# Modulation vectors of the next layer: the weighted sums moved from TensorE to GpSimd

## The reference, cut to what matters

```
silu_c  = silu(c)            # 1024 numbers, for the latent tokens
silu_cc = silu(c_ctx)        # 1024 numbers, for the context tokens
for i in range(4):
    mod_x = silu_c  @ w_mod[i] + b_mod[i]      # w_mod[i] is 1024 x 3072
    mod_c = silu_cc @ w_mod[i] + b_mod[i]
    shift, scale, gate = split(mod, 3)
    h = rms_norm(x, norm_g[i]) * (1 + scale) + shift
    ... mixer i ...
    x = x + gate * mixer_out
```

## Time and profile before

| | us |
|---|---|
| median of three runs | 8017.87 (8011.07 to 8035.23) |
| the profiled execution's own time | 8013.69 |
| its span, first to last instruction | 8011.9 |
| TensorE matmul busy | 6238.0, 78% |
| VectorE busy | 3114.6, 39% |
| ScalarE busy | 2047.2, 26% |
| GpSimd busy | 748.7, 9% |
| mean granted TensorE clock | 0.859 of full speed |

### The profile page before, as it was taken

How to read it: one execution, slowest core, us unless ns; L and a number is a source line. 1 busy time by engine, 2 the same in 40 slices (tenths; PEclk the granted TensorE clock), 3 DMA queues, 4 the chain that set the end, 5 groups by cost and what they waited for, 6 DMA issues and landing times. The chain is left out here.

```text
span 8011.9 us, 209544 instructions
## 1 busy us (share of the span) xinstructions
PE 6238.0 (78%) x90176; PEld 4264.4 (53%) x90176; DVE 3114.6 (39%) x7149; ACT 2047.2 (26%) x3566; POOL 748.7 (9%) x894
## 2 busy tenths in 40 slices
PE   5999777777778999888889350769699877777778
PEld 4555666666664555455445230544355566666664
DVE  3000455555551232255110689111310355555552
ACT  1000333333431111244011230210100244434440
POOL 0000222222220000000000000000000122222220
PEclk8999988888889899989988555569899988889988
DMA  3221000000002221221222305132111100000001
GB/s 104 85 91 68 25 16 16 16 16 16 16 8 100 86 88 61 79 63 43 100 78 85 48 31 45 47 76 83 64 71 66 43 16 16 16 16 16 16 16 63
DMA packets 172650, 401.84 MB, mean 50 GB/s; under 512 B 18752, under 2 KB 89280, under 8 KB 172224
## 3 DMA queue, kind: packets, MB, share of 16 engines
q1 hardware_dynamic: 137472, 297.39, 13.3%
q10 hardware_dynamic: 34752, 98.58, 3.0%
HBM read 286.86 MB, written 109.05 MB: 49 GB/s over the span
## 5 line engine op out<-in xcount | busy, mean ns | idle before, releaser
L278 PE MATMUL ps<-arena 128*128 128x512 f32 (+1 forms) x5824 | 2159.6, 533 | 249.6 <-DVE arena L1476 122.8
L278 PEld LDWEIGHTS ps<-arena 128*128 128x128 f32 x5824 | 1115.6, 192 | 1286.0 <-issue 1236.6
L1652 PE MATMUL ps<-arena 64*64 64x64 f32 x30720 | 639.2, 224 | 211.9 <-ACT arena L1924 119.6
L1652 PEld LDWEIGHTS ps<-arena 64*64 64x64 f32 x30720 | 549.8, 135 | 300.1 <-issue 293.1
L1924 ACT COPY arena<-ps 128x512 f32<-128x512 f32 (+1 forms) x800 | 497.6, 632 | 596.6 <-PE ps L1652 569.2
L486 PE MATMUL ps<-arena 128*128 128x512 f32 (+1 forms) x1152 | 425.5, 530 | 40.2 <-DMA arena<-na_w_in 40.2
L1982 POOL MEMSET arena<- 128x1024 f32 (+1 forms) x6 | 4.2, 739 | 4812.3 <-issue 4812.3
L1476 DVE SCALAR_TENSOR_TENSOR arena<-arena 128x1280 f32<-128x1280 f32 x96 | 141.3, 1547 | 635.4 <-PE ps L278 634.4
L1506 ACT COPY arena<-ps 128x1280 f32<-128x1280 f32 x64 | 78.4, 1225 | 1160.1 <-PE ps L278 1160.1
L486 PEld LDWEIGHTS ps<-arena 128*128 128x128 f32 x1152 | 220.8, 192 | 234.5 <-issue 223.3
L2104 DVE TENSOR_TENSOR arena<-ps,arena 128x512 f32<-128x512 f32 x480 | 302.5, 684 | 74.4 <-PE ps L1729 55.8
(11 more groups left out here) (252 smaller groups left out, 9954.3 us busy)
## 6 DMA issues: line engine op xcount, KB each, us to landing
proj<-arena ACTq DMA_DIRECT2D x104, 640.0 KB, 3.9
arena<-proj SPq DMA_DIRECT2D x104, 640.0 KB, 5.1
arena<-w_mod SPq DMA_DIRECT2D x96, 512.0 KB, 4.5
arena<-rw_w SPq DMA_DIRECT2D x68, 512.0 KB, 3.5
arena<-xres SPq DMA_DIRECT2D x40, 640.0 KB, 6.9
xres<-arena ACTq DMA_DIRECT2D x24, 640.0 KB, 6.5
arena<-na_w_in SPq DMA_DIRECT2D x24, 512.0 KB, 4.0
arena<-x SPq DMA_DIRECT2D x16, 640.0 KB, 6.7
```

The costliest lines, as they stand in the source:

```text
L278: last = nc.tensor.matmul(k.ps[:, 3 * u + n, 0:b - a], w[:, c * P:(c + 1) * P], src[:, c, a:b], start=(c == 0), stop=(c == KT - 1))
L1652: last = PE.matmul(part_of(out, dst, hh, g, d), part(l, src, hh, g, d), rhs, start=True, stop=True)
```

## The change

TensorE's eight two-column matmuls for a w_mod strip become two one-column matmuls. GpSimd first makes, for each of the two conditioning vectors, the weighted sum over the eight groups of input channels; TensorE sums that over the 128 partitions with a column of ones. GpSimd takes up the m strips of a turn when all m loads have landed, and TensorE's part waits for GpSimd (`weighted`) in place of the loads. A strip costs GpSimd twelve instructions and six drains: five multiplications (three over 4 x 128 elements of each partition, two over 2 x 128) and seven additions (one over 4 x 128, four over 2 x 128, two over 128). The second vector's products are written over the strip itself. SyncE's and VectorE's parts stay.

Besides, TensorE's program gets 153 `hold` instructions ahead of the recurrence's loop in layer 0 and 136 in layer 3.

```diff
 class HiddenModulation:
+        self.first, self.part, self.acc = k.arena.take(4, P), k.arena.take(2, P), k.arena.take(m, P)
+        self.weighted = es.semaphore("hm_weighted")
...
+    def pool_part(self, pool, i):
+        def times(out, strip, c, s):
+            n = out.shape[1]
+            self.nc.gpsimd.tensor_tensor(out, strip[:, c:c + n, :], self.k.cond[:, c:c + n, s:s + 1].to_broadcast([P, n, P]), ALU.mult)
+
+        def plus(out, a, b):
+            self.nc.gpsimd.tensor_tensor(out, a, b, ALU.add)
+
+        pool.wait_ge(self.w_in, i * (16 * self.m) + 16 * self.m)
+        hold(self.k, pool)
+        for q in range(self.m):
+            w = self.strips[:, q, :].rearrange("p (c o) -> p c o", o=P)
+            times(self.first, w, 0, 0)
+            times(self.part, w, 4, 0)
+            pool.drain()
+            plus(self.first[:, 0:2, :], self.first[:, 0:2, :], self.part)
+            pool.drain()
+            times(self.part, w, 6, 0)
+            pool.drain()
+            plus(self.first[:, 2:4, :], self.first[:, 2:4, :], self.part)
+            times(w[:, 0:4, :], w, 0, 1)
+            times(w[:, 4:8, :], w, 4, 1)
+            pool.drain()
+            plus(self.first[:, 0:2, :], self.first[:, 0:2, :], self.first[:, 2:4, :])
+            plus(w[:, 0:4, :], w[:, 0:4, :], w[:, 4:8, :])
+            pool.drain()
+            plus(self.acc[:, q, :], self.first[:, 0, :], self.first[:, 1, :])
+            plus(w[:, 0:2, :], w[:, 0:2, :], w[:, 2:4, :])
+            pool.drain()
+            plus(w[:, 0, :], w[:, 0, :], w[:, 1, :])
+        pool.drain().then_inc(self.weighted, 1)
+
     def tensor_part(self, pe, i):
-        pe.wait_ge(self.w_in, i * (16 * self.m) + 16 * self.m)
+        pe.wait_ge(self.weighted, i + 1)
         pe.wait_ge(self.ev, i + 1)
         for q in range(self.m):
-            for c in range(KT):
-                last = self.nc.tensor.matmul(self.k.ps[:, 6, 2 * q:2 * q + 2], self.strips[:, q, c * P:(c + 1) * P],
-                                             self.k.cond[:, c, :], start=(c == 0), stop=(c == KT - 1))
+            for s, sums in enumerate((self.acc[:, q, :], self.strips[:, q, 0:P])):
+                last = self.nc.tensor.matmul(self.k.ps[:, 6, 2 * q + s:2 * q + s + 1], sums, self.k.ones[:, 0:1], start=True, stop=True)
         last.then_inc(self.mm, 1)
...
 # in dense_to_dram, na_project and rwkv_project, each with its number of turns
+            @block.gpsimd
+            def _(pool):
+                with pool.Fori(0, turns) as i:
+                    hidden.pool_part(pool, i)
...
+LOOP_FILL = (153, 136)
...
 # in rwkv_recur
+            for _ in range(LOOP_FILL[j]):
+                hold(k, pe)
             pe.wait_ge(zeroed, 1)
             with pe.Fori(0, KT) as e:
```

More of the change, by code:

```diff
@@ L551, in _ @@
                 act.wait_ge(stored[u], 16 * 3 * KT // 2 + 16)
+        @block.gpsimd
+        def _(pool):
+            with pool.Fori(0, KT // 2) as pair:
+                hidden.pool_part(pool, pair)
         @block.vector
@@ L1454, in _ @@
                 turn(i)
+        if hidden:
+            @block.gpsimd
+            def _(pool):
+                with pool.Fori(0, hidden.turns) as i:
+                    hidden.pool_part(pool, i)
         @block.vector
```

## The result

The changed kernel takes 8091.74 us (median of 4 runs, 8084.70 to 8108.55), the kernel before beside it 8023.21 (4 runs, 8011.07 to 8035.23): ratio 1.0089, 95% interval 1.0066 to 1.0111. The profiled execution took 8084.70 us, that of before 8013.69: 71.0 more, at nearly the same mean clock (0.856 against 0.859).

What follows compares the result with a forecast made beforehand. The prediction took TensorE to bound the three projection phases. Layer 0's projection -25, `na_project` +107, S5 -26 and the fill +0.4 summed to +56 us on 8013.7; it said 8072 us, range 7985 to 8145.

Steps and rivals of the forecast that it cites:

- `na_project`: 16x16 attention's projection: GpSimd needs 65 us for six strips, TensorE waits 40 us a turn; +107 us in four turns.
- TensorE's saving in layer 0: Layer 0's projection: fewer matmul pairs save 31.4 us, a clock that stays up another 15; -46.4 us.
- The start: Layer 0's projection: GpSimd's first strips collide with VectorE's preparation, so TensorE starts 16 us later (ends: 0 and 20).
- The 5 us for turns in which VectorE makes `xs`: Layer 0's projection: in two turns GpSimd loses up to 12 us and uses up its margin; +5 us in all.
- A strip: GpSimd's cost for weighting one w_mod strip, drains included: 10.8 us, low end 7.8, high end 12.2.
- the 128x512 product near 1.28 us: Sign of being right: GpSimd's product of 512 elements per partition takes about 1.28 us; under 1 us would mean wrong.
- S5: S5's projection: GpSimd sets the pace with 32.4 us for three strips, turns of 40.3 us for 43.5; -26 us.
- The fill: Holds ahead of the recurrence's loops: 7.8 and 6.9 us, mostly covered by TensorE's wait for loads; +0.4 us.
- The recurrence's loop falls badly: Rival: moved instructions make all 64 recurrence windows as long as the first, 2.7 us each; +173, 8245 us; chance 0.04.
- dearer beside VectorE: Rival, `na_project`: VectorE's reciprocals hold GpSimd up, turns wait 8 to 16 us longer; 8105 to 8135; within the forecast's 0.68.
- no change: Rival: short GpSimd instructions cost less than their rows, a strip 9.7 us; 8019 us; chance 0.15.
- Faster: Rival: the repeated operand makes products cheaper, a strip under 8.9 us; 7981 us at 8.5; chance 0.13.

Runs made afterwards that it cites:

- e4: Changed kernel, with GpSimd in `rwkv_project` waiting for VectorE's first shifted copy before its first strip: 8093.29 us (one run).
- e3: Changed kernel, with `na_project`'s six w_mod strips issued after a turn's second row of weights instead of its last: 7928.73 us, ratio 0.9884 to the kernel before.
- e8: Changed kernel with holds under a wait, earlier `na_project` loads, later GpSimd start, and TensorE summing one of S5's three strips: 7876.85 us, 0.9812 of the kernel before.
- e2: Changed kernel, with the same holds moved to the head of TensorE's part of the projection, under an existing wait: 8054.69 us, ratio 1.0047 to the kernel before.

## Why the prediction was right

The forecast of 8072 us lay in the direction and of the size measured (8091.74), and the range held the result. The profiled executions differ by 71.0 us where the sum said 56. The mechanism that decides, GpSimd's lateness in `na_project`, is as forecast; that the total came so close is partly luck, since one term failed by 30 us and the others erred the other way. Point by point:

- **TensorE's saving in layer 0** held: -47.3 for -46.4, both parts of it, the fewer pairs and the clock that no longer falls.
- **The start** was +9.5 for +16. It was argued from rows of VectorE beside GpSimd, and the collision is there (2.04 us for 1.47), but the engines don't strictly alternate: VectorE loses 0.57 us an instruction where I took 0.82. With GpSimd held back (e4) the first strip is at 187.24 again, so the collision is the cause. The 5 us for turns in which VectorE makes `xs` didn't come: GpSimd lost 2.5 to 3.0 us there, not 12, and 8 us of margin held.
- **A strip** cost 10.04 to 10.4 us for 10.8, within 7%, by errors that partly cancel. The product was sized at 1.275 us and takes 1.04; the additions were sized at 1.098 and 0.644 and take 1.27 and 0.73. The rows I took the additions from read `eye2`, which repeats along the row: they were a cheaper form, and the product's row the dear one. The twelve instructions come to 9.4 us instead of 9.8, and the drains' gaps, less what neighbours overlap, to 0.6 instead of 1.0. The sign of being right "the 128x512 product near 1.28 us" failed. The Trainium skill's rate (GPSIMD Engine Reference, section 3.1) came to 9.4 us by the estimate, measured is 10.04. The additions here take 0.19 us and 2.11 ns an element, which at the section's 2048 elements would be 4.5 us, an estimate that agrees with its 4497 ns; what the estimate of 9.4 lacked is the fixed part.
- **`na_project`**: +96.2 for +107, with a wait of 36 us for 40, turns 24 us longer for 27, and GpSimd as the releaser. The six strips took 62.6 us for the 68 reckoned, but GpSimd began them 12.0 us after the first issue instead of 10.1. This was the deciding term, and e3 shows it as a cause: with the strips issued earlier the wait is gone and the term turns from +96.2 into -60.9 us (-67.5 + 6.6 at the phase's two ends against before).
- **S5**: -20.8 for -26, and +3.6 in phases behind it for which I had no term. I took the strips to land 5.7 us after their issue, every turn; it is 6.6 in the short turns and 9.1 to 10.7 in the long ones. That GpSimd sets the pace here held, and e8 shows it.
- **The fill is the step that failed.** "A `hold` takes 51 ns: 153 take 7.8 us" used the busy time of an instruction that stood alone as its pace in a row. In a row they come every 0.15 us: 23.3 us, of which 8.7 were covered, so +16.6 in layer 0 and +14.1 in layer 3, 30.7 in place of 0.4. e2 shows it as a cause: with the same holds under a wait the 31 us are gone. The other terms were too high together. From the 56 of the sum to the 71 measured: fill +30.3, S5 +5.2, `na_project` -10.8, start -6.5, layer 0's turns -5.9 (the 5 us that didn't come among them), and +2.6 for the stretches between.
- **"The recurrence's loop falls badly"** didn't happen in the changed kernel, and had 0.04. But the mechanism is real, its price is higher than I gave it (190 and 219 us in the two layers, not 173 for both), and it comes as a step, not as 2.7 us on every window. What I called a fill that "nearly restores the place" is what keeps 200 us away.

The rival "dearer beside VectorE" did not come as it was put: beside the reciprocals GpSimd ran at its own pace, and what it lost to VectorE's two-operand work was 2.4 us a turn, not 8 to 16. The rival "no change" was nearer than the result looks. It was given to strips of 8.9 to 10.1 us, and S5's take 10.04; by my own weights (24 us in each of the two phases for a microsecond of a strip) 10.4 in `na_project` and 10.04 in S5 come to about 8045, hardly above the 0.3% that I called no change. The late landings and the fill made up for it. "Faster" needed strips under 8.9 us, and none was.

## What to carry to other kernels

Work moved to an idle engine is free only where its inputs are there early enough; here the same GpSimd work cost 96 us in one phase and won 61 there once its loads were issued earlier in the turn, so ask first when the data lands and move that too. Price a run of small control instructions by how far apart they start, not by how long each is busy, and put such a run under a wait that exists anyway. Any change to the number of instructions ahead of a long loop can move it over a border beyond which part of each iteration is fetched anew (here some four more packets of 16 KB a window), so look at an iteration's time and at the instruction queue's packets before and after.

## What the hardware showed that I had not expected

- Semaphore increments on TensorE's queue, 51 ns busy each, start 0.15 us apart (153 in 23.3 us).
- On GpSimd a two-operand instruction of 512 elements per partition takes 1.27 us with two different full operands and 1.04 with a repeated number or the same part twice; of 256, 0.73 and, with a repeated number, 0.61. Multiplication and addition cost the same.
- GpSimd and VectorE slow each other when both run instructions with two tile operands (VectorE's 2.04 us instead of 1.47, GpSimd's product of 256 1.68 instead of 0.61); beside VectorE's reciprocal of 8.15 us GpSimd lost nothing.
- A loop of 1620 TensorE instructions runs at 22 us or at 25 to 34 us an iteration by its place in the program alone, the slow way with 255 to 273 packets of instructions loaded in a recurrence instead of 102 to 110, and 109 instructions that cost no time where they stand made the kernel 4.7% slower.
- Three 512 KB loads land 9.1 to 10.7 us after the first issue in turns where another is issued 1.25 to 2.0 us ahead, and 6.6 us where it is issued 7.9 us or more ahead; that the one ahead is the cause was read from the rows, not tried, and one turn (0.55 us ahead, 8.6 us) doesn't fit it alone.
